# The last projection with tokens on partitions

## The reference, cut to what matters

```
merged = gate_a * (y_a @ w_proj_a) + gate_b * (y_b @ w_proj_b)   # [512, 1024]
y = merged @ w_out                                               # [512, 1024]
x = x + gate * rms(y, g_post)                                    # rms over the 1024 features
```

## Time and profile before

| | |
|---|---|
| median of 3 runs | 1488.11 us |
| the profiled execution's own time | 1492.32 us |
| its span (first to last record) | 1489.6 us |
| mean granted TensorE clock | 0.987 |
| busy: PE, DVE, ACT, POOL | 96%, 54%, 32%, 10% |
| last matmul of `out2` to the end of the span | 1471.87 to 1489.6 us |

### The profile page before, as it was taken

The page is one execution under the profiler, slowest core; times in us unless marked ns, Lnnn a source line. Parts: engine busy times, 40 slices in busy tenths (PEclk is TensorE's granted clock), DMA queues, the critical chain, the costliest instruction groups (busy, mean ns, idle before and its releaser), DMA issues.

```text
span 1489.6 us, 21131 instructions
## 1 busy us (share of the span) xinstructions
PE 1433.7 (96%) x9168; PEld 1127.6 (76%) x9168; DVE 800.0 (54%) x1091; ACT 484.1 (32%) x716; POOL 148.4 (10%) x142
## 2 busy tenths in 40 slices
PE   7999999999999999998999999999999999999995
PEld 5676686877868788875877787877888877778784
DVE  6464554645547854534464555545435435566654
ACT  5321223414134443233431221223333232663321
POOL 2120300202010020000200000000140011003012
PEclk9999999999999999999999999999999999999998
DMA  5110201102014225320244524222222322221221
GB/s 192 43 44 30 72 30 44 58 30 72 31 62 170 94 98 163 111 68 17 97 178 167 178 99 170 99 92 100 91 79 71 103 89 99 71 71 70 87 99 71
DMA packets 37644, 134.32 MB, mean 90 GB/s; under 512 B 4121, under 2 KB 5785, under 8 KB 36528
## 3 DMA queue, kind: packets, MB, share of 16 engines
q1 hardware_dynamic: 31824, 113.00, 22.5%
q0 software_dynamic: 1680, 14.39, 2.7%
q10 hardware_dynamic: 4048, 5.59, 1.1%
HBM read 130.86 MB, written 2.10 MB: 89 GB/s over the span
## 4 chain that ended last, share of the span: by engine, by line
PE 67%; issue 15%; DVE 8%; ACT 5%; DMA 4%; POOL 2%; ACTq 0%; POOLq 0%; DVEq 0%
PE bank L381 65%; DMA w_raw<-panels 3%; ACT w_hi L799 1%; DVE tmp L1284 1%; PE bank L384 1%; DVE w_lo L1284 1%; POOL acc L1131 1%; ACT scores L799 1%; ACT L799 1%; POOL tmp L1131 1%; DMA xT<-x 1%; DVE ada_sum L1292 0%; DVE xT L1284 0%; ACT opA_hi L799 0%; DVE mem_lo L1292 0%
## 5 line engine op out<-in xcount | busy, mean ns | idle before, releaser
L381 PE MATMUL bank<-opA_hi,w_hi 128*128 128x512 f32 x1104 | 459.8, 417 | 14.3 <-DVE opA_lo L1292 8.9
L1284 DVE TENSOR_TENSOR w_lo<-w_raw,w_hi 128x1024 fp32r<-128x1024 f32 (+1 forms) x211 | 259.9, 1232 | 367.0 <-ACT w_hi L799 367.0
L381 PE MATMUL bank<-opA_hi,w_lo 128*128 128x512 f32 x1104 | 439.0, 398 | 0.0
L381 PE MATMUL bank<-opA_lo,w_hi 128*128 128x512 f32 x1104 | 438.9, 398 | 0.0
L799 ACT ACTIVATE w_hi<-w_raw 128x1024 fp32r<-128x1024 f32 (+1 forms) x211 | 222.0, 1052 | 435.0 <-DMA w_raw<-panels 434.7
L381 PEld LDWEIGHTS bank<-opA_hi,w_hi 128*128 128x128 f32 x1104 | 208.9, 189 | 75.7 <-issue 22.7
L381 PEld LDWEIGHTS bank<-opA_hi,w_lo 128*128 128x128 f32 x1104 | 209.0, 189 | 50.8
L381 PEld LDWEIGHTS bank<-opA_lo,w_hi 128*128 128x128 f32 x1104 | 209.5, 190 | 44.6 <-issue 2.2
L381 PE MATMUL bank<-opB_hi,w_hi 128*128 128x512 f32 x448 | 178.4, 398 | 1.7 <-DVE w_lo L1284 1.1
L381 PE MATMUL bank<-opB_hi,w_lo 128*128 128x512 f32 x448 | 177.2, 396 | 0.0
L381 PE MATMUL bank<-opB_lo,w_hi 128*128 128x512 f32 x448 | 177.2, 395 | 0.0
(11 more groups left out here) (281 smaller groups left out, 1435.8 us busy)
## 6 DMA issues: line engine op xcount, KB each, us to landing
w_raw<-panels SPq DMA_DIRECT2D x210, 512.0 KB, 3.4
ada_w<-ada POOLq DMA_DIRECT2D x8, 1536.0 KB, 7.7
xT<-x ACTq DMA_DIRECT2D x1, 2048.0 KB, 11.8
out<-xT SPq DMA_DIRECT2D x8, 256.0 KB, 2.0
memT<-mem ACTq DMA_DIRECT2D x1, 1024.0 KB, 14.4
xT<-x SPq DMA_DIRECT2D x3, 256.0 KB, 7.5
xT<-x ACTq DMA_DIRECT2D x3, 256.0 KB, 7.8
mats<-mat POOLq DMA_DIRECT2D x1, 672.0 KB, 4.9
```

Source lines behind the costliest of these rows:

```text
L381: return pe.matmul(o, lhsT, rhs, start=start, stop=stop, skip_group_check=True)
L1284: return ve.tensor_tensor(o, a, b, op)
```

## The change

`out2` is computed with tokens on the partitions. The stationary operand is now a 128-token slice of the activations `opA`, the moving one is half a k-tile row of the weights: 512 output features. So a loaded "panel" of `out2` is now one k-tile (128 input features by all 1024 outputs), and the result is four token blocks by two halves, in eight PSUM banks (`TOKEN_BANKS`). The first 5 k-tiles are multiplied one after the other over all eight banks; the last 3 are done bank by bank, so that the banks are finished one after the other. Of these last three panels the very last has a slot of its own (in `P`) and is loaded right after panel `out2`+3.

The sum of squares is now along the free dimension: ACT's Square gives it by `accum_out`, and the reciprocal root is a column. `gate2` must lie along the free dimension: 16 matmuls of an identity slice with `gate2` broadcast as stationary operand make it in banks 6 and 7 before `merge2`, and DVE copies it to `gate_row`. x3 must have tokens on partitions: DVE transposes each of its 8 tiles in 32x32 blocks (`x3_blocks`, two tiles at the end of each of the first four `merge2` panels), and 16 transfers of 128 KB on SP's queue, four behind each of the first four `out2` panels' loads, put the blocks in place (`x3_tok`). The output's columns come in the order `OUT_ORDER`, which the host undoes. POOL has no work left at the end.

```diff
--- before.py
+++ after.py
 RW_ALONE, RW_LORA = 4, 8
@@ -115,6 +115,7 @@
 F_WKV_END = F_WKV - (F_START + F_NORM + F_AB + F_X + 10 * F_SOLVE + 2 * F_Z + 2 * NC * F_CHAIN + 1 + F_TAIL + F_TAIL2)
 F2_MAX, F2_SOFTMAX, F2_OUT, F2_LAST = 8, 10, 3, 14
 F2_COPY, F2_NORM = 6, 8
+TOKEN_BANKS = ((4, 5), (6, 7), (0, 2), (1, 3))
 F2_MID = 16 * KT - 2 - 4 * (F2_MAX + F2_SOFTMAX + F2_OUT) - F2_LAST
 
...
+    w_raw.append(place("w_raw_last", [NP, KT, NP], r_p + 2 * TB))
+    w_lo.append(place("w_lo_last", [NP, KT, NP], r_p + 2 * TB, F32R))
+    w_hi.append(place("w_hi_last", [NP, KT, NP], r_p + 4 * TB, F32R))
...
+    x3_blocks = place("x3_blocks", [NP, 4 * FT, KT, 32], r_p + UB * TB)
+    x3_tok = place("x3_tokens", [NP, FT, D], r_p + ZA * TB)
+    gate_row = place("gate_row", [NP, D], r_p)
+    square_sums, root_cols = cols[:, 0:8], cols[:, 56:60]
...
-    raw_here = [sem(f"raw_panel_in_slot{j}") for j in range(W)]
+    raw_here = [sem(f"raw_panel_in_slot{j}") for j in range(W + 1)]
     hi_made, lo_made, multiplied = sem("panel_high_made"), sem("panel_low_made"), sem("panel_multiplied")
     left = [sem(f"bank{j}_left") for j in range(2)]
+
+    def slot(i):
+        return i % W if i < N_PANELS - 1 else W
...
         p.steps(F2_LAST)
-        p.to(None)
-        pe.wait_ge(summed, 4 * KT)
-        token_sums(acc, bank[7])
-        token_spread(rstd, bank[6], 3)
+        pe.wait_ge(ada_cols, 6)
+        pe.wait_ge(ws_done, 1)
+        pe.wait_ge(sv_step, 4)
+        for k in range(KT):
+            for b in range(2):
+                ins = mm(bank[6 + b][:, :].rearrange("p (b k l) -> p b k l", b=2, k=KT)[:, :, k, :],
+                         gate2[:, k:k + 1].broadcast_to([NP, NP]),
+                         mat("ident")[:, b * 64:(b + 1) * 64].rearrange("p (b l) -> p b l", b=2))
+        ins.then_inc(ws_mm, 1)
+        p.to("out2")
+
+        def out_product(t, h, k):
+            w = slot(FIRST["out2"] + k)
+            o, tokens = bank[TOKEN_BANKS[t][h]][:, :], slice(t * NP, (t + 1) * NP)
+            hi, lo = (x[w][:, 4 * h:4 * h + 4, :].rearrange("p k n -> p (k n)") for x in (w_hi, w_lo))
+            mm(o, opA[0][:, k, tokens], hi, k == 0, False)
+            mm(o, opA[1][:, k, tokens], hi, False, False)
+            return mm(o, opA[0][:, k, tokens], lo, False, k == KT - 1)
+
+        for k in range(KT - W):
+            pe.wait_ge(lo_made, made(FIRST["out2"] + k))
+            pe.wait_ge(op_lo, OPERAND["out2"] + k + 1)
+            for t in range(4):
+                if k == 0 and t == 1:
+                    pe.wait_ge(ws_done, 3)
+                if k == 0 and t >= 2:
+                    pe.wait_ge(left[t - 2], left_after(FIRST["out2"] - 4 + t))
+                for h in range(2):
+                    ins = out_product(t, h, k)
+            ins.then_inc(multiplied, 1)
+        pe.wait_ge(lo_made, made(N_PANELS - 1))
+        pe.wait_ge(op_lo, OPERAND["out2"] + KT)
+        for t in range(4):
+            for h in range(2):
+                for k in range(KT - W, KT):
+                    ins = out_product(t, h, k)
+                ins.then_inc(out_mm, 1)
...
         def high(i):
-            w = i % W
-            ac.wait_ge(raw_here[w], 16 * (i // W + 1))
+            w = slot(i)
+            ac.wait_ge(raw_here[w], 16 * (i // W + 1) if w < W else 16)
...
-            elif name == "out2":
-                ac.wait_ge(multiplied, i + 1)
-                if m >= 2:
-                    ac.wait_ge(summed, 3 * KT + m - 1)
-                act(sq[j][:, :], bank[j][:, :], ACT.Square).then_inc(squared, 1)
...
-        token_root(head_cols[:, 0:4], 3)
+        for t in range(4):
+            for h in range(2):
+                ac.wait_ge(out_mm, 2 * t + h + 1)
+                act(sq[h][:, :], bank[TOKEN_BANKS[t][h]][:, :], ACT.Square, scale=D ** -0.5,
+                    accum_out=square_sums[:, 2 * t + h:2 * t + h + 1]).then_inc(squared, 1)
+            token_root(root_cols[:, t:t + 1], 3 + t)
...
-                n = {"mix": 0, "xo": KT, "out2": 3 * KT}[name] + m
+            elif name in ("mix", "xo"):
+                n = {"mix": 0, "xo": KT}[name] + m
                 if m == 0:
                     gp.wait_ge(cleared, CLEAR[name])
-                accumulate(acc[:, :], sq[j][:, :], (squared, KT + n + 1 + (KT if name == "out2" else 0)), summed, 1 + n)
...
-        gp.wait_ge(weigh_mm, 2 * XH + 4)
-        gp.memset(acc[:, :], 0.0).then_inc(cleared, 1)
-        p.to(None)
-        gp.wait_ge(x3_made, KT)
-        for n, k in enumerate((0, 2, 4)):
-            gp.wait_ge(sv_step, 12 + k + 1)
-            tt(xT[:, k, :], xT[:, k, :], P[:, k, :], ALU.add).then_inc(last_add, 1)
...
+                if not one and m < 4:
+                    ve.wait_ge(x3_made, KT)
+                    for k in range(2 * m, 2 * m + 2):
+                        ve.transpose(x3_blocks[:, :, k, :], xT[:, k, :].rearrange("p (t l) -> p t l", l=32)).then_inc(x3_made, 1)
...
-            elif name == "out2":
-                ve.wait_ge(squared, 5 * KT + m + 1)
-                ts(P[:, m, :], ps, gate2[:, m:m + 1], ALU.mult).then_inc(left[j], 1)
...
         p.steps(F2_LAST)
+        ve.wait_ge(ws_mm, 2)
+        for b in range(2):
+            ve.tensor_copy(gate_row[:, b * S:(b + 1) * S], bank[6 + b][:, :]).then_inc(ws_done, 1)
         p.to(None)
-        ve.wait_ge(tok_mm, 3)
-        ts(head_cols[:, 0:4], bank[7][:, 0:4], EPS, ALU.add).then_inc(tok_var, 1)
-        token_reciprocal(head_cols[:, 0:4], 2)
-        token_wide(head_cols[:, 0:4], rstd)
-        ve.wait_ge(tok_spread, 3)
-        for k in range(KT):
-            tt(P[:, k, :], P[:, k, :], bank[6][:, :], ALU.mult).then_inc(sv_step, 1)
-            if k not in (0, 2, 4):
-                ve.wait_ge(sv_step, 12 + k + 1)
-                tt(xT[:, k, :], xT[:, k, :], P[:, k, :], ALU.add).then_inc(last_add_v, 1)
+        ve.wait_ge(x3_here, 16 * 16)
+        for t in range(4):
+            rc = root_cols[:, t:t + 1]
+            for h in range(2):
+                n = 2 * t + h
+                ve.wait_ge(squared, 5 * KT + n + 1)
+                if h:
+                    ts(rc, square_sums[:, n - 1:n], square_sums[:, n:n + 1], ALU.add, EPS, ALU.add).then_inc(tok_var, 1)
+                if t:
+                    ve.wait_ge(out_made, n - 1)
+                tt(tmp[h][:, :], bank[TOKEN_BANKS[t][h]][:, :], gate_row[:, h * S:(h + 1) * S], ALU.mult).then_inc(gated, 1)
+            token_reciprocal(rc, 2 + t)
+            for h in range(2):
+                ve.wait_ge(gated, 2 * t + h + 1)
+                o = x3_tok[:, t, h * S:(h + 1) * S]
+                stt(o, tmp[h][:, :], rc, o, ALU.mult, ALU.add).then_inc(out_made, 1)
 
     def sync_program():
         sy = nc.sync
-        for i in range(N_PANELS):
+
+        def panel(i):
+            sy.dma_start(w_raw[slot(i)][:, :, :].rearrange("p k n -> p (k n)"), panels[i, :, :]).then_inc(raw_here[slot(i)], 16)
+
+        for i in range(N_PANELS - 1):
             if i >= W:
                 sy.wait_ge(multiplied, i - W + 1)
-            sy.dma_start(w_raw[i % W][:, :, :].rearrange("p k n -> p (k n)"), panels[i, :, :]).then_inc(raw_here[i % W], 16)
+            panel(i)
             if i == 0:
                 for k in (1, 4, 7):
                     sy.dma_start(xT[:, k, :], x_in[k * NP:(k + 1) * NP, :]).then_inc(x_here[k], 16)
-        for k in range(KT):
-            if k in (0, 2, 4):
-                sy.wait_ge(last_add, k // 2 + 1)
-            else:
-                sy.wait_ge(last_add_v, (0, 1, 0, 2, 0, 3, 4, 5)[k])
-            sy.dma_start(out[k * NP:(k + 1) * NP, :], xT[:, k, :]).then_inc(stored, 16)
+            if FIRST["out2"] <= i < FIRST["out2"] + 4:
+                f = i - FIRST["out2"]
+                sy.wait_ge(x3_made, 2 * KT)
+                for q in range(4):
+                    sy.dma_start(x3_tok[32 * q:32 * q + 32, :, f * 256:(f + 1) * 256],
+                                 x3_blocks[32 * f:32 * f + 32, q:4 * FT:4, :, :].rearrange("p t k l -> p t (k l)")
+                                 ).then_inc(x3_here, 16)
+                if f == 3:
+                    panel(N_PANELS - 1)
+        for t in range(4):
+            for h in range(2):
+                sy.wait_ge(out_made, 2 * t + h + 1)
+                sy.dma_start(out[t * NP:(t + 1) * NP, h * S:(h + 1) * S], x3_tok[:, t, h * S:(h + 1) * S]).then_inc(stored, 16)
         sy.wait_ge(stored, 16 * KT)
...
+OUT_ORDER = np.arange(D).reshape(KT, 4, 32).transpose(1, 0, 2).reshape(-1)
...
-                             panelled(i["w_out_2"][0])])
+                             i["w_out_2"][0][:, OUT_ORDER].reshape(KT, NP, D)])
...
-    out = nc.dram_tensor("out", (D, S), F32, kind="ExternalOutput").ap()
+    out = nc.dram_tensor("out", (S, D), F32, kind="ExternalOutput").ap()
...
-    return np.ascontiguousarray(got.T)[None]
+    return np.ascontiguousarray(got[:, np.argsort(OUT_ORDER)])[None]
```

(24 more changed lines are left out.)

2 lines of the change are left out of this document (1 added, 1 removed).

## The result

The changed kernel takes 1482.18 us (median of 20 runs, 1478.91 to 1496.6) against 1488.8 us of the kernel before (median of 20 runs, 1487.31 to 1501.8). The ratio is 0.9947, with a 95% interval of 0.9930 to 0.9963: 0.5% faster, about 8 us. The two medians alone lie 6.6 us apart, 0.4%. The forecast was 1480 us and 0.5%.

The account below looks back on a forecast made before the run. TensorE was taken as the bound, busy 1433.7 of 1489.6 us, with a nearly idle 17.7 us tail. Terms -12.1 + 2.5 + 1.5 = -8.1 gave 1480 us on the median's scale; range 1476 to 1486.

Parts of the forecast that it names:

- tail: After the last out2 matmul: 5.6 us to the span's end instead of 17.7, a gain of 12.1 us.
- gate row: Before merge2: 16 narrow float32 matmuls of 3.7 us, partly in a 1.2 us TensorE wait, cost +2.5 us.
- last three panels: Near out2's end: TensorE waits for low parts of panels 6 and 7, +1.5 us, bounds 0.3 and 2.2.
- transposes: Eight on VectorE in the first four merge2 panels, taken as 0.69 us each: cost nothing, within 4.0 us of slack.
- transfers: 16 of 128 KB on SP's queue, four behind a panel's load: taken to cost nothing.
- upper bound of 6.6: After the last matmul: 6.6 us if a table load of 1.28 us comes back before the last root.
- lower bound of 5.3: After the last matmul: 5.3 us if stores don't meet, with start-to-start steps of 0.61.
- -12.4 to -11.1: Span of the tail's gain, in us, used for the forecast's own range.
- only panel 6 late: Lower bound of the stall in out2's last three panels: 0.3 us if panel 7's low part adds no delay.
- 5.4 us of slack: In out2: a weight panel is ready 5.8 us after its load's issue and wanted 11.2 after it.
- The rival: TensorE's clock falls after the gate row or panel stall: 1.4 to 2.5 us a fall; chance 0.18.
- the argument that kept its chance low: Against a clock fall: the 1.5 us panel stall is shorter than a 1.87 us idle that was borne.

## Why the prediction was right, step by step

**Result and mechanism.** 1482.2 in place of 1480; ratio 0.9947 in place of 0.9946 (1480 by 1488.1). Of the 2.2 us between, 0.7 are in the scale: the kernel before took 1488.8 beside it, not 1488.1. No run explains the other 1.5; single runs of the changed kernel differ by more. The stretches are the sharper test: -8.8 where -8.1 was forecast.

| term | forecast | measured | seen in |
|---|---|---|---|
| tail | -12.1 (left 5.6) | -12.6 (left 5.13) | both traces |
| gate row | +2.5 | +2.3, of it 2.0 by the row | its omission |
| last three panels | +1.5 | +1.55 (stall 1.33) | the two orders, the slots |
| transposes | 0, at 0.69 each | 0, at 0.687 each | three times as many |
| transfers | 0 | 0, behind the panels | queue of GpSimd |

**The tail.** The order came as forecast: square, column, bank product (only its last 0.30 behind the column), reciprocal, two products of 1.41 together. No table load before the last root: it came once, before the first root at 1467.11, beside TensorE. That excludes the upper bound of 6.6. The term was a little too large: the last store is issued 3.1 us behind the last matmul (1482.09) where 3.4 was forecast, and it takes 2.05 us as it was taken to, without the 0.2 us for stores that meet. So 5.13 lies below the lower bound of 5.3, and -12.6 outside -12.4 to -11.1. That the six other banks are off the path is shown by the kernel that finishes them 0.7 us apart: there they are on it, and the tail is 10.33.

**The gate row.** The size, 3.68 us for 32 records, is the 3.7 of the forecast, and that columns hardly matter is now shown in both directions: 1.84 for 16 of one column, 3.68 for 32 of 64, 1.95 for 16 of 128. The rows show no extra cost of a broadcast stationary operand. What the forecast didn't have is a price of 0.3 us that stays when the row is left out. No trace names what it is.

**The last three panels.** The stall is where it was put, 72 matmuls before the end, released by VectorE. Its reason, a low part behind another one, was tested from three sides: with the order turned 0.26 is left (forecast for "only panel 6 late": 0.3), with a slot for both no stall, with the last load in its turn 5.91. The block had +1.55 for a stall of 1.33, and the other 0.2 us are at the same place: from start to start the matmuls before and behind the wait are 1.73 us apart (1460.18, 1461.91) in place of 0.23, and the next one comes 0.33 behind, 0.1 more than the usual step. That makes 1.6. The idle time of the row is shorter, since it counts from the modelled end of a matmul.

**The transposes.** One row of the profile after settles the most uncertain price:

```profile
L1429 DVE STREAM_TRANSPOSE x_blocks<-xT 128x512 f32<-128x512 f32 x8 | 5.2, 687 | 0.0
```

0.687 us each, which is the tensor operation's row, not the copy's 0.43 or the reciprocal's 3.35. The Trainium skill, VectorE: DVE Perf Modes, The three transpose paths, gives 311 ns for 128x128 of bf16; the estimate from four of these, 1.24, is too long by 0.55, and the measurement decides. The other page that bears on it, Vector Engine (DVE) Microarchitecture Reference, 3.8, says that the transposing front-end is pipelined to sustain one element per cycle and lane; that the eight rows cost what VectorE's tensor operations of 128x512 do (0.68 to 0.69) agrees with this.

**The transfers.** Right in the sum, wrong in a part: SP's issue of one takes 0.60 us, not 0.33, so four take 2.4 and not 1.3. They landed 3.8 to 5.1 us after the issue, and the `out2` panels beside them in 4.0 to 4.3, where all panels have 3.5. All of that lies in the 5.4 us of slack. The forecast said why they are hidden (the slack of a panel behind a group of four), and the same 16 in one burst from GpSimd are not.

**The clock.** It stayed at 1.00 behind the row in all nine traces that have one, and behind the stall of 1.2 to 1.4 us in all six. The rival came true where longer waits were made: 0.50 behind 5.91 us, for 2.3 us, and 0.50 behind 2.48 us in the kernel with three transposes. But the argument that kept its chance low, that 1.87 us of idle had been borne, doesn't hold. The same wait stands in the changed kernel run again, and there the clock fell behind it (a row of its timeline, then a window):

```profile
1239.82 0.66 PE L395 MATMUL bank<-mats,P 128*128 128x128 f32 x4 [1.87 <-DVE rotated L1321]
...
1242.00:1244.00 2.00, 2.00 (x6) 1.52 (x6) 1.90 (x3) 0.55 (x1) 0.20 (x1) 0.50 0.00 0
```

In the kernel with one k-tile bank by bank, on the other hand, 2.83 us of idle ahead of a matmul at 833.42 were borne. So the length of the idle alone doesn't decide, and a stall of 1.33 is not shown to be safe, only to have been borne six times.

The Trainium skill, TensorE: Matmul & The Clock Gate, Part 1, says that the throttled clock is the default and that activity releases it; 16 or 32 narrow records without a fall agree with that. What narrow records do to the clock by themselves stays open. The fall around 1110 us is in all eleven traces, among records of one column, with no idle of TensorE over 1.3 us in that stretch. There narrow records and waits of TensorE follow each other from 1105.85 to 1119.08, while the gate row is one piece of 3.7 us with dense matmuls directly before and behind it. No run separates the narrow records from the waits.

## What to carry to other kernels

When the last block of work is bound by TensorE, look at what runs after its last matmul, and put the reduction on the axis in which an engine adds along the free dimension; then finish the banks one by one over as many k-tiles as make a bank slower than the engines that drain it, and check that the operands of these k-tiles can be there at once. The cost of that order is a wait for the last of them, and here a slot of its own for each of the last two panels removed it. Small transfers beside a stream of loads were free one group behind each load, and not in one burst from another queue.

## What the runs showed of the hardware beside this

- A float32 product with a 128x128 stationary operand costs TensorE 0.115 to 0.122 us per record and two records, whether 1, 64 or 128 columns move, at the full clock. So the widest one is the cheapest per column. At 0.50 16 records of one column took 3.41 to 3.55 us in place of 1.84.
- The time of a run goes with TensorE's granted clock. In twelve runs of the changed kernel on one chip, the eight with a mean clock of 0.989 to 0.994 took 1479.4 to 1483.4 us, the four with 0.982 to 0.985 1487.3 to 1490.4. That is about as much as the whole change brings, and the traces show falls in stages that the change doesn't touch. Stretches of a trace told more here than its time.
- An issue on SP's queue costs 0.33 us for a store of 256 KB and 0.60 for a transfer of half the bytes in pieces of 1 KB between partitions of SBUF. The traces don't tell whether the pieces or the two ends inside SBUF make the difference.
